# x by columns for the first layer's products, x by rows behind the third weight unit, the halved root directly behind the root

## What is computed

```python
D_MODEL = 1024; SEQ = 256; DEPTH = 2; IN_COLS = 4096

def rmsnorm(x, g, eps=NORM_EPS):
    xf = x.astype(jnp.float32)
    y = xf * lax.rsqrt(jnp.mean(xf * xf, axis=-1, keepdims=True) + eps)
    return (y * g.astype(jnp.float32)).astype(x.dtype)

def first_block(x, norm_g, w_in, ...):
    for l in range(DEPTH):
        h = rmsnorm(x, norm_g[l])
        proj = h @ w_in[l]
        ...          # q, k, v, gate of a windowed attention (out_a) and of a differential one (out_b)
        y = jnp.concatenate([out_a * silu(g_a), out_b * silu(g_b)], axis=-1)
        x = x + y @ w_out[l]
    return rmsnorm(x, final_g)
```

## Time and profile before

| | us |
|---|---|
| median of 3 runs | 1177.98 |
| lowest and highest | 1177.89, 1178.29 |
| the profiled execution | 1177.49 |
| its span in the trace | 1175.7 |
| TensorE busy in it | 1155.3 |

### The profile page before, as it was taken

How to read it: one execution, slowest core, us unless ns; L and a number is a source line. 1 busy time by engine, 2 the same in 40 slices (tenths; PEclk the granted TensorE clock), 3 DMA queues, 4 the chain that set the end, 5 groups by cost and what they waited for, 6 DMA issues and landing times.

```text
span 1175.7 us, 15187 instructions
## 1 busy us (share of the span) xinstructions
PE 1155.3 (98%) x5640; PEld 945.4 (80%) x5640; DVE 835.9 (71%) x1179; ACT 583.2 (50%) x764; POOL 562.9 (48%) x417
## 2 busy tenths in 40 slices
PE   9999999999999999899999999999999999999998
PEld 6787787877788888888887888888888887888887
DVE  7897578966897797678779667797793666654423
ACT  5557564676543442644343277443442756443440
POOL 1366324584364452734535228665351553545360
PEclk9999999999999999999999999999999999999999
DMA  9976479846799997569898568798874534876550
GB/s 353 354 274 225 135 252 332 277 161 223 238 368 319 342 347 273 187 216 343 276 338 319 218 234 283 245 346 300 321 277 142 197 115 161 268 245 193 207 197 36
DMA packets 183832, 297.91 MB, mean 253 GB/s; under 512 B 8464, under 2 KB 102352, under 8 KB 183760
## 3 DMA queue, kind: packets, MB, share of 16 engines
q1 hardware_dynamic: 177696, 284.82, 70.2%
q10 hardware_dynamic: 6064, 12.14, 3.1%
HBM read 294.79 MB, written 2.13 MB: 253 GB/s over the span
## 4 chain that ended last, share of the span: by engine, by line
PE 83%; DVE 8%; ACT 4%; issue 2%; SPq 1%; DMA 1%; POOL 1%; ACTq 0%; DVEq 0%
PE ps L1903 25%; PE ps L1916 25%; PE ps L1908 25%; PE ps L2196 2%; PE ps L1996 2%; DVE w_lo L1232 1%; ACT w_hi L665 1%; DVE ps L1216 1%; DMA raw<-w_in 1%; PE ps L2053 1%; POOL stat L525 1%; SPq L492 1%; PE ps L2042 1%; DVE ps L1328 1%; DVE x L1329 1%
## 5 line engine op out<-in xcount | busy, mean ns | idle before, releaser
L534 POOL TENSOR_TENSOR w_lo<-raw,w_hi 128x512 fp32r<-128x512 f32 x348 | 485.0, 1426 | 419.0 <-ACT w_hi L665 419.0
L665 ACT ACTIVATE w_hi<-raw 128x2048 fp32r<-128x2048 f32 x188 | 354.5, 1910 | 100.1 <-PE ps L1916 65.3
L1903 PE MATMUL ps<-w_hi,h_hi 128*128 128x512 f32 x1120 | 312.1, 400 | 1.1 <-issue 0.8
L1916 PE MATMUL ps<-w_lo,h_hi 128*128 128x512 f32 x1120 | 301.6, 391 | 1.6 <-DVE w_lo L1232 1.0
L1908 PE MATMUL ps<-w_hi,h_lo 128*128 128x512 f32 x1120 | 300.3, 390 | 0.0
L1232 DVE TENSOR_TENSOR w_lo<-raw,w_hi 128x2048 fp32r<-128x2048 f32 x96 | 224.7, 2346 | 100.5 <-ACT w_hi L665 98.4
L1916 PEld LDWEIGHTS ps<-w_lo,h_hi 128*128 128x128 f32 x1120 | 209.1, 188 | 50.0 <-DVE w_lo L1232 3.3
L1908 PEld LDWEIGHTS ps<-w_hi,h_lo 128*128 128x128 f32 x1120 | 210.2, 188 | 45.7 <-DVE h_lo L1292 0.2
L1903 PEld LDWEIGHTS ps<-w_hi,h_hi 128*128 128x128 f32 x1120 | 201.8, 188 | 43.5 <-issue 5.5
L1216 DVE SCALAR_TENSOR_TENSOR ps<-ada_raw,ccol,ps 128x512 f32<-128x512 f32 x240 | 181.1, 754 | 7.9 <-DMA ada_raw<-ada_w 1.1
L956 ACT ACTIVATE a_hi<-ps 128x512 fp32r<-128x512 f32 x44 | 26.4, 599 | 153.8 <-PE ps L2196 153.8
(11 more groups left out here) (208 smaller groups left out, 963.6 us busy)
## 6 DMA issues: line engine op xcount, KB each, us to landing
raw<-ffn_in SPq DMA_DIRECT2D x176, 512.0 KB, 5.9
ada_raw<-ada_w SPq DMA_DIRECT2D x144, 512.0 KB, 7.1
raw<-ffn_out SPq DMA_DIRECT2D x44, 1024.0 KB, 6.0
raw<-w_in SPq DMA_DIRECT2D x31, 1024.0 KB, 7.9
raw<-w_out SPq DMA_DIRECT2D x8, 1024.0 KB, 5.1
ada_raw<-kv_ada_w SPq DMA_DIRECT2D x16, 512.0 KB, 8.0
raw<-w_kv SPq DMA_DIRECT2D x8, 1024.0 KB, 5.8
raw<-w_q SPq DMA_DIRECT2D x4, 1024.0 KB, 5.1
```

The costliest lines, as they stand in the source:

```text
L534: ins = pool.tensor_tensor(w_lo[:, u % RAW, piece], raw[:, u % RAW, piece], w_hi[:, u % RING, piece].bitcast(F32), ALU.subtract)
L665: act.activation(w_hi[:, u % RING, :], raw[:, u % RAW, :], ACT.Copy).then_inc(*S.inc("w_hi_ready", u))
L1903: pe.matmul(bank(b), hi[:, k_in_lhs + k, tok], wh[:, k, c * 512:(c + 1) * 512], start=start and k == 0, stop=False)
L1916: ins = pe.matmul(bank(b), hi[:, k_in_lhs + k, tok], wl[:, k, c * 512:(c + 1) * 512], start=False, stop=stop and k == nk - 1)
```

## The change

The host also passes x transposed (`x_cols`, 1024 x 256). It is loaded in two halves of 512 KB (four 128-row blocks each, runs of 1 KB) into the buffer `hn`, seen as `x_T`. `h_hi` and `h_lo` of the first layer are made from `x_T` in SBUF: the first half by VectorE for each tile, the second by ScalarE for both tiles in one instruction per block. TensorE's 16 transposes of x are gone, and the four warm-up matmuls are in one piece. x by rows, two loads of 512 KB, comes behind weight unit 2 and ahead of unit 3; its squares go to another buffer. VectorE halves the root directly behind the root, ahead of `lows(4)`. So ScalarE's eight instructions of 128 columns for the second half of `h_hi` (L845) become four of 256.

```diff
@@ sync
-            sp.dma_start(x[:, 0, :], x_in[0:P, :]).then_inc(x_in_sem[0], 16)
+            def x_columns(half):
+                rows = x_cols[512 * half:512 * half + 512, :].rearrange("(k p) n -> p k n", p=P)
+                sp.dma_start(x_T[:, 4 * half:4 * half + 4, :], rows).then_inc(x_cols_in[half], 16)
...
                 if u == 0:
-                    for k in range(0, 4, 2):
-                        sp.dma_start(into[:, k:k + 2, :], parts[0][:, k:k + 2, :]).then_inc(
-                            raw_in[0] if k else half_in, 16)
+                    sp.dma_start(into[:, 0:2, :], parts[0][:, 0:2, :]).then_inc(half_in, 16)
+                    x_columns(0)
+                    sp.dma_start(into[:, 2:4, :], parts[0][:, 2:4, :]).then_inc(raw_in[0], 16)
...
                 if u == 0:
-                    sp.dma_start(x[:, 1, :], x_in[P:2 * P, :]).then_inc(x_in_sem[1], 16)
+                    x_columns(1)
+                if u == 2:
+                    for t in range(NT):
+                        sp.dma_start(x[:, t, :], x_in[t * P:(t + 1) * P, :]).then_inc(x_in_sem[t], 16)
@@ scalar, first_norm
+                act.wait_ge(x_cols_in[1], 16)
+                for k in range(4, KC):
+                    ins = act.activation(h_hi[:, k, :], x_T[:, k, :], ACT.Copy, scale=scale[:, k:k + 1])
+                ins.then_inc(*S.inc("h_hi_second"))
...
-                fill(1)
+                fill(2)
                 act.wait_ge(*S.at("stat_filled"))
                 for t in range(NT):
                     act.wait_ge(x_in_sem[t], 16)
-                    act.activation(hn[:, t, :], x[:, t, :], ACT.Square, accum_out=st(t)).then_inc(
+                    act.activation(squares_at[:, t, :], x[:, t, :], ACT.Square, accum_out=st(t)).then_inc(
                         *S.inc("squares_ready", "a0", t))
-                    fill(2 + t)
                 fill(4)
@@ vector, first_norm
+                dve.wait_ge(x_cols_in[0], 16)
                 for t in range(NT):
-                    dve.wait_ge(*S.at("xT_done", "a0", t, 0))
-                    tok, b = slice(t * P, (t + 1) * P), job_bank["xT_done", "a0", t, 0]
-                    dve.tensor_tensor(h_hi[:, 0:4, tok], bank(b).rearrange("p (k c) -> p k c", k=4),
+                    tok = slice(t * P, (t + 1) * P)
+                    dve.tensor_tensor(h_hi[:, 0:4, tok], x_T[:, 0:4, tok],
...
-                lows(4)
                 dve.wait_ge(*S.at("rsqrt_ready", "a0"))
                 dve.tensor_scalar(st(2, NT), st(0, NT), 0.5, None, ALU.mult).then_inc(*S.inc("half_root_ready"))
+                lows(4)
                 fill(3)
@@ tensor
-            warm_up(WARM_UP[0])
+            warm_up(WARM_UP)
...
-                if layer == 0:
-                    norm_T(name, 0)
-                    warm_up(WARM_UP[1])
...
-                    if s == 0 and not layer:
-                        norm_T(name, 1)
```

More of the change, by code:

```diff
@@ L65 @@
               ("up", 1, 1): {40: ("down", 1, 1)}}
-WARM_UP = (3, 1)
+WARM_UP = 4
 SUM_STEPS = (5, 7, 9, 11, 12, 14, 15, 18, 22, 31)
@@ L198, in column_fill, with program @@
     return {0: 2 * (s // 4) + 2, 1: 2 * (s // 4) + 3}.get(s % 4)
-def program(nc, known, x_in, w_in, w_out, ffn_in, ffn_out, pool_w, w_kv, w_q, w_o, ada_w, kv_ada_w,
+def program(nc, known, x_in, x_cols, w_in, w_out, ffn_in, ffn_out, pool_w, w_kv, w_q, w_o, ada_w, kv_ada_w,
             norm_cols, ada_b_cols, c_cols, na_bias, t5_bias, lam_rows, sub_cols, qk_rows,
@@ L295, in program @@
         qk_stage = hn[:, :, 0:512]
+        x_T = hn.rearrange("p t d -> p (t d)").rearrange("p (k c) -> p k c", k=KC)
         ffn_tanh = hn[:, 0, 0:512].rearrange("p (t c) -> p t c", t=NT)
@@ L346, in program @@
         stores = [name for steps in ROW_STORES.values() for name in steps.values()]
+        x_cols_in = [ctx.enter_context(nc.semaphore(f"x_cols_loaded{i}")) for i in range(2)]
         half_in = ctx.enter_context(nc.semaphore("first_half_loaded"))
@@ L832, in first_norm @@
                 scale, _ = norm_cols_of("a0")
+                squares_at = pr1.rearrange("p w t k -> p (w t k)").rearrange("p (t d) -> p t d", t=NT)
                 act.wait_ge(half_in, 16)
@@ L840, in first_norm @@
                 act.wait_ge(first_in, N_FIRST)
+                act.wait_ge(x_cols_in[1], 16)
+                for k in range(4, KC):
+                    ins = act.activation(h_hi[:, k, :], x_T[:, k, :], ACT.Copy, scale=scale[:, k:k + 1])
+                ins.then_inc(*S.inc("h_hi_second"))
                 for t in range(NT):
[L842 to L847, removed]
-                fill(1)
+                    S.same("h_hi_ready", ("a0", t, 1), "h_hi_second", ())
+                fill(2)
                 act.wait_ge(*S.at("stat_filled"))
@@ L1335, in first_norm, with first_low @@
                 scale, _ = norm_cols_of("a0")
[L1337 to L1341, removed]
+                def first_low(half, *tiles):
+                    tok = slice(tiles[0] * P, (tiles[-1] + 1) * P)
+                    for t in tiles:
+                        dve.wait_ge(*S.at("h_hi_ready", "a0", t, half))
+                    for kk in range(4 * half, 4 * half + 4):
                         ins = dve.scalar_tensor_tensor(
-                            out=h_lo[:, kk, tok], in0=bank(b)[:, k * P:(k + 1) * P], scalar=scale[:, kk:kk + 1],
+                            out=h_lo[:, kk, tok], in0=x_T[:, kk, tok], scalar=scale[:, kk:kk + 1],
                             in1=h_hi[:, kk, tok].bitcast(F32), op0=ALU.mult, op1=ALU.subtract)
-                    ins.then_inc(*S.inc("h_lo_ready", "a0", t, half))
+                    ins.then_inc(*S.inc("h_lo_first", half, tiles[0]))
+                    for t in tiles:
+                        S.same("h_lo_ready", ("a0", t, half), "h_lo_first", (half, tiles[0]))
+                dve.wait_ge(x_cols_in[0], 16)
                 for t in range(NT):
-                    dve.wait_ge(*S.at("xT_done", "a0", t, 0))
-                    tok, b = slice(t * P, (t + 1) * P), job_bank["xT_done", "a0", t, 0]
-                    dve.tensor_tensor(h_hi[:, 0:4, tok], bank(b).rearrange("p (k c) -> p k c", k=4),
+                    tok = slice(t * P, (t + 1) * P)
+                    dve.tensor_tensor(h_hi[:, 0:4, tok], x_T[:, 0:4, tok],
                                       scale[:, 0:4].unsqueeze(2).broadcast_to([P, 4, P]), ALU.mult).then_inc(
@@ L1353, in first_norm @@
                     S.same("h_hi_ready", ("a0", t, 0), "h_hi_first", (t,))
-                    first_low(t, 0)
+                    first_low(0, t)
                     lows(0)
-                for t in range(NT):
-                    first_low(t, 1)
+                first_low(1, 0, 1)
                 lows(2)
@@ L2139, in between @@
                 def between(s):
-                    if s == 0 and not layer:
-                        norm_T(name, 1)
+                    pass
                 def freed(g):
@@ L2429 @@
     arrays = {
-        "x_in": get("x").reshape(T, D)[order],
+        "x_in": get("x").reshape(T, D)[order], "x_cols": get("x").reshape(T, D)[order].T,
         "w_in": get("w_in"), "w_out": get("w_out"), "ffn_in": get("ffn_w_in_2"), "ffn_out": get("ffn_w_out_2"),
```

## The result

The changed kernel takes 1182.49 us in the median of 6 runs (1181.21 to 1183.27), the kernel before 1178.03 us in the median of its 6 (1177.34 to 1178.29). The ratio is 1.0036, with a 95% interval of 1.0026 to 1.0047: slower by 4.46 us, where 4.5 was forecast. The profiled execution took 1182.95 us, 5.46 more than that of before.

The account below looks back on a forecast made before the run. Bound: TensorE, 98% busy, held at the first queries' transposes by a chain from weight unit 4's landing. 1177.49 + 2.85 (load 2.95, root -0.1) + 1.7 (clock) = 1182.0 profiled; median 0.49 above, 1182.5 us; range 1179.2 to 1183.5.

Parts of the forecast that it names:

- The bound: TensorE, 98% busy, and a chain from unit 4's landing reach the first queries' transposes (29.13) together; the later sets the time.
- Part 1, the load: One more MB queued ahead of weight unit 4: its `w_hi` starts 2.95 us later, at 24.44.
- Part 2, the halved root: Halved root leaves the chain between unit 4's `w_lo` and `lambda_dots`: worth about 0.1 us; its new place costs nothing.
- Part 3, the front: Transposes gone, first product possible at 6.7, L1916 0.1 earlier to 0.5 later; all hidden in the wait for L2042.
- Part 4, the clock: After TensorE's pause of about 3.1 us the granted clock falls, costing 1.7 us (bounds 0 and 1.7).
- The case without the clock: Rival: same delay, but the clock stays at 2.4 GHz through the pause; 1180.8 us, chance 0.30.
- The sum: Transposes L2042 start 2.85 us later, plus 1.7 for the clock: 1182.0 profiled, 1182.5 us median.
- Absorbed: Rival: TensorE's later wait (1.08 us at 100.24) swallows delay; 1179.3 to 1180.3; chance 0.12 together with not reaching the bound.
- The front running free: Rival: without the transposes the first half steps run ahead, L2042 starts 3.0 us earlier; 1175.0 us, chance 0.05.
- A gap in the queue that takes the MB: Rival: unit 4 lands within 0.5 us of before; 1178 +- 0.5; chance 0.12 together with absorbed.

Follow-up runs that it names:

- the second kernel above: Changed kernel with only VectorE's work on the constants (`lambda_dots`) moved ahead of `w_lo` of unit 4; 1180.97 us (1.0025 times the kernel before).
- the first: Changed kernel with the constants' work ahead of unit 4 on both VectorE and ScalarE; 1180.19 us (1.0024 times the kernel before).
- the third: Changed kernel with VectorE's constants' work ahead of `w_lo` of unit 4 and x by columns in 4 KB runs; 1179.37 us (1.0021).

## Why the prediction was right, step by step

**The bound** was right: a chain that starts from unit 4's landing. With the additional MB alone it moved as with the change, and with the constants' work taken off it the pause went.

**Part 1, the load.** The term was 2.95, and unit 4's `w_hi` was put at 24.44. The profiled execution had 25.39, 0.95 more. Of its 3.90 the runs show 2.58 for the MB and 0.43 for runs of 1 KB (I had 2.51 and 0.46). The remaining 0.9 is what the step lacked: it took one trace's landing as fixed. Four traces of kernels with the change's loads have unit 4's `w_hi` at 24.80, 24.81, 25.28 and 25.39, and four with before's loads ahead of it have 21.49, 21.58, 22.11 and 22.16. The shift is there by the third load: in the four with the change's loads, unit 4's `w_hi` stands 16.9 us behind that of unit 0's second half (L847), which starts at 7.93, 7.94, 8.42 and 8.53. Against the two earliest 0.3 of the 0.9 stays; the order of the first four loads differs, and was not tried alone. What moves the first loads is open. In the median the delay alone is 2.98 us, by the run with four matmuls on zeros.

**Part 2, the halved root:** right. It was put at 0.1 us of the chain and gave 0.06 alone and 0.08 in the changed kernel, and its new place cost nothing: VectorE had halved the root at 20.76 and stood still for unit 3's `w_hi` until 22.68.

**Part 3, the front.** Right in that it is hidden, wrong in two sizes. The first product was put at 6.7 and came at 8.64: `x_T` was there at 7.24 and not at 6.0, and `h_hi` took 1.30 us and not 0.6. It couldn't have come at 6.7 in any case. The fourth warm-up matmul was given 0.86 us for two passes, its time at 6.83, but at the place to which it moved one pass takes 0.86 us (the warm-up's weight loads start at 5.03, 5.88 and 6.74), and TensorE was through with it at 7.84. L1916 of half step 0 came 0.86 us later, where 0.1 earlier to 0.5 later was given; half step 2's came 0.48 later, within its 0.5. The rule cited from the Trainium skill, "SBUF — State Buffer", section "SBUF: two separate sides", that a VectorE instruction with two SBUF inputs and a GpSimd instruction that reads SBUF lock each other out, is borne out by the rows again, 1.30 beside 0.68 us for the same instruction, and on GpSimd's side by 2.95 beside 2.54 us. It cost nothing at the end, since the pause swallowed it. TensorE's last matmuls ahead of the pause start at 28.38, 0.39 later than before, and an estimate of what the whole front would cost without a pause is that 0.39.

**Part 4, the clock.** The stretch at half the clock came, and cost 1.58 us at TensorE's next waits; 1.7 was taken from one row at 488 us. With TensorE kept busy it was gone and the end 1.7 us earlier. What I had not said is that it doesn't fall in every execution. Of the change's six runs two lie at 1181.2 and 1181.5, with a mean granted clock of 0.998, and four at 1182.2 to 1183.3, with 0.997. The kernel with the MB ahead of unit 3 splits in the same way, two runs and four, 1.3 us apart. The five runs with x in 4 KB runs all have 0.997, and none of the fourteen in which the pause was filled has less than 0.998. The case without the clock, 1180.8, was thus not wrong but the less frequent one.

**The sum.** In the profiled execution the delay was larger than forecast by 0.97, and the end 5.46 us later and not 4.55. In the median the two terms are 2.98 and about 1.5, against 2.85 and 1.7. That the median meets the forecast to a hundredth is luck: the sum had an error of some tenths in each term.

**The rivals.** Absorbed: out, the later waits kept their length. (Its upper end, + 2.3, doesn't follow from its own terms: 2.85 less 1.08 is 1.8.) The front running free: out, unit 4 came later. A gap in the queue that takes the MB: out, by the additional MB alone.

## What to carry to other kernels

Where loads stand in one queue that is full, ask of a new load what stands behind it, and go through all of its users: here unit 4 was the first that had no slack, and VectorE's steps at 34 to 37 us, with the weights that they need, the second, where the MB still cost 1.4 us. Taking 16 transposes off the busiest engine brought nothing here: its new front took 0.39 us longer even so, and it had to wait for a landing behind that. A pause of 3 us on TensorE cost its length and, in most executions, another 1.3 to 1.6 us by the clock. Where the clock falls in some executions only, compare those with the same mean granted clock: two medians here were 1.6 us apart, and like with like 0.3.

## What the hardware showed that I had not expected

The clock's fall depends on the execution and not on the pause's length alone: it fell behind a wait of 2.36 us (the second kernel above) and not behind waits of 2.36 us (the first) and 2.53 us (the third), and within one kernel some runs have it and some not. The landing of the first loads moves too: with the same first loads, unit 0's first half was there for ScalarE at 4.85 to 5.52 and its second half at 7.93 to 8.53, not in step with the first, and what hangs on the later loads moved with the second. And a matmul of 128x512 on fp32 zeros is two passes, of 0.43 us each at 29 to 35 us, so that as a filler four, not eight, cover 3.4 us; in the warm-up one pass takes 0.86 us, though the profile gives 1.00 as the granted clock in both places.
